# The opening of a two-layer trunk: scale's modulation units first, four separate signals, shift's units last

## The chip, the cores and the metric

The kernel runs on one core of a Trainium2 chip. The metric is the device time of one execution in microseconds; the time of a kernel is the median of its runs. The profile shows one execution, instruction by instruction.

## What is computed

The reference is a two-layer trunk (model width 1024) over 256 context and 256 latent tokens. What matters here is how each layer begins:

```python
mod = jax.nn.silu(c) @ w_mod[i] + b_mod[i]
mod_c = jax.nn.silu(c_ctx) @ w_mod[i] + b_mod[i]
sh1, sc1, g1, sh2, sc2, g2 = jnp.split(mod[:, None, :], 6, axis=-1)
h = _modulate(_rmsnorm(x, norm1_g[i]), sh1, sc1)      # h * (1 + scale) + shift
...
y, yc = _mixer(h, hc, ...)                            # begins with h @ w_in[i]
x = x + g1 * y
...
x = x + g2 * _peer(h2, ...)                           # 128*128 experts
```

So the first projection of layer 0 needs the RMS of x (a mean of squares over the 1024 channels of each token), the scale sc1 (which goes into the gain) and the shift sh1. w_mod of a layer is 1024 x 6144 floats. The kernel holds it as 24 units of 1 MB, four to each of the six parts: units 0 to 3 give sh1, units 4 to 7 give sc1.

## The kernel before

All weights come through `ring`, four slots of 1 MB each. Unit u goes into slot u % 4. SyncE (SP) issues every load in program order; ahead of the load of unit u it waits until the slot's `used` counter says that the unit before it in that slot has been read by TensorE. Each slot has its own arrival signal, `unit_in`. The stages follow each other in one list: `mod`, `norm1`, `front`, `s5`, `ret`, `merge`, `norm2`, `route`, `gates`, `experts`, twice, and `final`. The change touches `mod` and the first `norm1`.

Before, SP issues three loads on one signal, `const_in`: `cst` (378.5 KB), `par` (188 KB: biases, gains, the two condition vectors, the S5 parameters) and `xT` (2 MB). TensorE, ScalarE and VectorE all start by waiting for 48, that is for all three. Then SP streams w_mod units 0 to 7 (`stream`, L648), the last four behind the slots' `used`.

The engines in stage `mod`, layer 0, in their program order:

- **ScalarE**: silu of the condition (L1552) and its copy into `cond0` (L1529); eight squares of `xT` into `hT` (`squares`, L1481); an Exp chain of small parameter operations with VectorE (L1555 to L1563), which needs three loads of function tables; the Sqrt of the mean (`stddev`, L1487); then `mod_rows`, which copies the row of each modulation unit out of PSUM into `mrow0` (L1536), eight copies.
- **TensorE**: `norm_mean`, eight products with a matrix of 1/1024 (16 instructions of 512 columns, two for each product) into PSUM bank 7; `mod_rows`, for each of eight units eight products (16 instructions of 256 columns) into bank k; `mod_columns`, 16 products (32 instructions of 2 columns) that turn the rows of shift and scale into columns in bank 4.
- **VectorE**: the small parameter chain (L2042 to L2077); `inverted`, the reciprocal of the deviations in `rs1` (L1987); `mod_tables`, which adds the bias (L2006) and makes the gain out of the scale (L2012, L2013).

Stage `norm1` and the first unit of `front` then run as a pipeline over the eight channel blocks k:

- **VectorE** scales in place (`normed`, L1998, two instructions to a block, signal `h_scaled`), subtracts for the low part of the first weight unit (`front_low`, L2021), and makes the low part of h (`loP`, L2087).
- **ScalarE** first copies the first front unit to its rounded form (`front_high`, L1515), then adds the shift (`shifted`, L1499, output `hiP`, signal `h_ready`).
- **TensorE** makes the first projection in three parts: high weights by `hiP` as its blocks come, low weights by `hiP`, high weights by `loP`. Its last instruction frees the front unit's slot.

In `front` SP's loads interleave: one front unit, two late modulation units, and so on, each into a slot that TensorE must have freed. Every load, and every wait, behind this point hangs on the events before it; none is tied to an absolute time.

`count(eng, s, n)` waits for a semaphore with a credit that VectorE adds at its start (4 for `mod_row`), so a row's bank can be written before a copy was made.

Of the kernel before, what the change touches and what calls it, by code (L numbers as in the profile page):

```python
# [22 lines left out]
P = 128  # L23
DM = 1024
# [158 lines left out]
def x_for(st, k):  # L183

    if st[0] == "norm2":
        return X_COUNT[st] - OUT_UNITS + k // 2 + 1 if st[2] else X_COUNT[st]
    return X_COUNT[st] - KD + k + 1
# [7 lines left out]
def passes_done(st):  # L195

    return sum(s[0] == "experts" for s in STAGES[:STAGES.index(st)])
# [30 lines left out]
def norms_before(st):  # L228
    return [s for s in STAGES if s[0] in ("norm1", "norm2", "final")].index(st)
# [28 lines left out]
def build_program(nc, a, until=None):  # L258
    stages = STAGES if until is None else STAGES[:until]
    ctx = ExitStack()  # L260
    with ctx:
# [3 lines left out]
        def sem(name):  # L265
            return ctx.enter_context(nc.semaphore(name))
# [205 lines left out]
        ps = ctx.enter_context(nc.psum_tensor("ps", [P, 8, 512], F32))  # L472


        const_in = sem("const_in")
        unit_in = [sem(f"unit_in{s}") for s in range(RING)]
        u_in = [sem(f"u_in{s}") for s in range(RING)]
        keys_in = sem("keys_in")
# [104 lines left out]
        def count(eng, s, n):  # L583

            eng.wait_ge(s, n + CREDIT[s.name])
# [45 lines left out]

        @block.sync
        def _(sp):
            sp.dma_start(cst[:, :], a["consts"]).then_inc(const_in, 16)
            sp.dma_start(par[:, :], a["params"]).then_inc(const_in, 16)
            sp.dma_start(xT[:, :, :], a["x_t"]).then_inc(const_in, 16)

            def load(u, src, i=None, per=0):
                n = u // RING
# [8 lines left out]
            def stream(u, src, count):  # L648

                head = RING if u < RING else 0  # L650
                for k in range(head):
                    load(u + k, src[k])
                turns_ = (count - head) // RING
                with sp.Fori(0, turns_) as i:
                    for k in range(RING):
                        load(u + head + k, src[bass.ds(i * RING + (head + k), 1)].rearrange("o p n -> (o p) n"), i, RING)
# [43 lines left out]
            for st in stages:  # L700
                kind, l, h = st
                u = BASE[st]
                if kind == "mod":
                    stream(u, a["w_mod"][0, 0:EARLY], EARLY)
                elif kind == "front":
                    for k in range(FRONT_UNITS):
                        load(u + front_at(l, k), a["w_front"][l, k])
# [176 lines left out]

        @block.tensor
        def _(pe):
            pe.wait_ge(const_in, 48)

            def mm(out, w, x, start, stop, **k):
                return pe.matmul(out, w, x, start=start, stop=stop, **k)  # L890
# [1 line left out]
            def norm_mean(st, sqb, w):  # L892
                n = norms_before(st)
                for k in range(KD):

                    pe.wait_ge(sq_ready, KD * n + k + 1)
                    last = mm(ps[:, mean_bank(st), 0:w], cst[:, C_ONES_D:C_ONES_D + P], sqb[:, k, :], k == 0, k == KD - 1)
                last.then_inc(mean_ready, 1)
# [13 lines left out]
            def mod_rows(u, l, first, n, bank, cond):  # L912

                with pe.Fori(0, n // RING) as i:
                    for k in range(RING):
                        mod_row_of(u + k, l * MOD_UNITS + first + k, bank + k, cond, i)

            def mod_columns(l, s0, s1, row, bank, begin=0):

                count(pe, mod_row, l * MOD_UNITS + MOD_UNITS // 6 * s1)  # L920
                for c in range(s0 * KD, s1 * KD):
                    at = (c - begin * KD) * P
                    last = mm(ps[:, bank, 2 * c:2 * c + 2], row[:, at:at + P], cst[:, C_SEL:C_SEL + 2], True, True)
                last.then_inc(mod_col, 1)

            for st in stages:
                kind, l, h = st
                u = BASE[st]
                if kind == "mod":


                    norm_mean(("norm1", 0, 0), hT, TL)
                    pe.wait_ge(cond_ready, 1)
                    mod_rows(u, 0, 0, EARLY, 0, cond0)
                    mod_columns(0, 0, 2, mrow0, 4)
                elif kind == "norm1" and l:
                    norm_mean(st, sq1, TL)
                elif kind == "norm2":
# [531 lines left out]
        @block.scalar  # L1470
        def _(act):
            own = Chain(act, act_own)
            act.wait_ge(const_in, 48)

            def squares(st, sqb, lo, w):
                for k in range(KD):
                    if st != STAGES[1]:
                        act.wait_ge(x_ready, x_for(st, k))
                    if k == KD // 2 and passes_done(st):
                        act.wait_ge(x_back, 16 * passes_done(st))  # L1480
                    act.activation(sqb[:, k, :], xT[:, k, lo:lo + w], ACT.Square).then_inc(sq_ready, 1)  # L1481

            def stddev(st, rs, w):
                n = norms_before(st)

                act.wait_ge(mean_ready, n + 1)
                act.activation(rs[:, 0:w], ps[:, mean_bank(st), 0:w], ACT.Sqrt, bias=eps).then_inc(std_ready, 1)  # L1487

            def shifted(st, dst, w, lo, row):

                n = norms_before(st)
                for k in range(KD):
                    act.wait_ge(h_scaled, KD * n + k + 1)
                    for hf in range(w // 256):
                        side = hf if w > 256 else lo // CTX
                        s = slice(hf * 256, hf * 256 + 256)
                        d = dst[:, k, s]
                        src = d if row else by_four_of(scaled(st[1], k, s))
                        last = act.activation(d if row else by_four(hiP[:, k, :], s), src, ACT.Identity,  # L1499
                                              bias=modT[:, st[1], row, k, side:side + 1])  # L1500
                    last.then_inc(h_ready, 1)
# [46 lines left out]
            for st in stages:  # L1548
                kind, l, h = st
                u = BASE[st]  # L1550
                if kind == "mod":
                    own.link(act.activation(par[:, N_C:N_C + 16], par[:, N_C:N_C + 16], ACT.Silu))  # L1552
                    filled(cond0, 1)
                    squares(("norm1", 0, 0), hT, 0, TL)
                    own.link(act.activation(lg[:, :], par[:, N_DEC:N_DEC + 16], ACT.Exp))  # L1555
                    own.link(act.activation(lg[:, :], lg[:, :], ACT.Copy, scale=-1.0))

# [3 lines left out]
                    act.activation(sp_(S_SIN), sp_(S_T1), ACT.Sin)  # L1561
                    act.activation(sp_(S_COS), sp_(S_T2), ACT.Sin, scale=-1.0,
                                   bias=cst[:, C_HPI:C_HPI + 1]).then_inc(s5_trig, 1)  # L1563
                    stddev(("norm1", 0, 0), rs1, TL)
                    mod_rows(u, mrow0, 0, EARLY, 0)
                elif kind == "norm1":
                    if l:
                        squares(st, sq1, 0, TL)
# [10 lines left out]
                elif kind == "front":  # L1579
# [32 lines left out]
                            act.activation(pmag, pmag, ACT.Exp)  # L1612
                            act.activation(r8[:, :], s5p[:, S_LR, l * NG:(l + 1) * NG], ACT.Exp, scale=8.0).then_inc(pow_trig, 1)
                    if l == 0:
                        act.wait_ge(mod_col, 2)
                        act.activation(mcol[:, :], ps[:, 6, 2 * 2 * KD:2 * 5 * KD], ACT.Copy).then_inc(mod_out, 1)
                elif kind == "s5":
                    lo, hi = layer_width(l)
# [356 lines left out]
        def _(dve):  # L1975
            own = Chain(dve, dve_own)
            link = own.link
            v = nc.vector
            dve.wait_ge(const_in, 48)
            for s_ in (mod_row, gate_ready, gate_ps, w_ready):  # L1980
                dve.sem_inc(s_, CREDIT[s_.name])

# [1 line left out]
            def inverted(st, rs, w):  # L1984

                dve.wait_ge(std_ready, norms_before(st) + 1)
                link(v.reciprocal(rs[:, 0:w], rs[:, 0:w]))  # L1987

            def normed(st, rs, w, dst, lo, gains, done):

                if st != ("norm1", 0, 0):
                    inverted(st, rs, w)
                for k in range(KD):
                    for hf in range(w // 256):
                        side = hf if w > 256 else lo // CTX
                        s_ = slice(hf * 256, hf * 256 + 256)
                        d = dst[:, k, s_] if dst is not None else scaled(st[1], k, s_)
                        last = v.scalar_tensor_tensor(d, xT[:, k, lo + hf * 256:lo + hf * 256 + 256],  # L1998
                                                      gains(k, side), rs[:, s_], ALU.mult, ALU.mult)
                    last.then_inc(done, 1)  # L2000
# [34 lines left out]
            for st in stages:  # L2035
                kind, l, h = st
                u = BASE[st]
                if kind == "mod":
# [36 lines left out]
                    link(v.tensor_tensor(sp_(S_T1), sp_(S_COS), li, ALU.mult))  # L2075
                    link(v.tensor_tensor(sp_(S_T0), sp_(S_T0), sp_(S_T1), ALU.subtract))
                    link(v.tensor_tensor(sp_(S_BI), sp_(S_T0), sp_(S_T2), ALU.mult))  # L2077
                    inverted(("norm1", 0, 0), rs1, TL)
                    mod_tables(0, 0, 2, ps[:, 4, 0:4 * KD], 1)
                elif kind == "norm1":  # L2080
                    normed(st, rs1, TL, None, 0, lambda k, s: gain[:, l, 0, k, s:s + 1], h_scaled)
                    front_low(l, 0)
# [57 lines left out]
                elif kind == "s5":  # L2140
# [69 lines left out]

                    def skips():

                        dve.wait_ge(mod_col, 2)
                        v.tensor_tensor(dsk[:, :, :], cst[:, C_DIAG:C_DIAG + 16].unsqueeze(1).to_broadcast([P, 16, 16]),
                                        par[:, N_D:N_D + 16].unsqueeze(2).to_broadcast([P, 16, 16]), ALU.mult).then_inc(d_ready, 1)

# [60 lines left out]
                elif kind == "ret":  # L2277
# [84 lines left out]
                    out_low(1)  # L2362
                    if l == 0:
                        dve.wait_ge(mod_out, 1)
                        mod_tables(0, 2, 5, mcol[:, :], 2)
                elif kind == "merge":
                    lo, hi = layer_width(l)
                    w_ = hi - lo
# [32 lines left out]
                elif kind == "route":  # L2401
# [72 lines left out]
                                               nth[:, 0:k, c].unsqueeze(1).to_broadcast([P, 2, k, hw]), ALU.is_equal)  # L2474
                    link(last)
                    if next_route(st):
                        mod_tables(0, 5, 6, ps[:, 3, 10 * KD:12 * KD], 3)
                        mod_tables(1, 0, 2, ps[:, 2, 0:4 * KD], 4)
                        normed(next_route(st), rs2, 256, h2T, 0, lambda k, s: gain[:, l, 1, k, s:s + 1], h_scaled)
                    tops = topf[:, :, :, :, :].rearrange("p s k t h -> p (s k) (t h)").unsqueeze(2)  # L2480
                    late_ = eq[:, :, :, hw:2 * hw].rearrange("p s k (j m) -> p (s k) j m", j=TOPK // 2)
# [34 lines left out]
                    half = next_mod(st)  # L2516
                    if half:
                        s0, s1 = MOD_PARTS[st]
                        mod_tables(1, s0, s1, ps[:, 2, 2 * s0 * KD:2 * s1 * KD], 4 + half)
                elif kind == "gates":  # L2520
                    gb = groups_before(st)
                    idxT = peer_tiles(l)[1]
# [259 lines left out]
```

## Time and profile before

| | us |
|---|---|
| median of 3 runs | 2964.58 |
| lowest, highest | 2958.05, 2966.55 |
| profiled execution, its own time | 2967.0 |
| its span, first to last instruction | 2965.2 |

Of the span TensorE is busy 92 per cent, VectorE 83, ScalarE 48, GpSimd 16. The profiled execution's own time stands 1.8 us over its span. Starts in the rows further down are counted from the span's start. "SPq" is SyncE's queue with its DMA issues, "PEld" the load of weights into TensorE. A figure in square brackets is the engine's idle time ahead of the row and what ended it.

### The profile page before, as it was taken

The page shows a single profiled execution, that of the slowest core. Times are in us where ns is not written, and L with a number is a line of the kernel's source. Part 1 is how long each engine was busy: PE and PEld are TensorE (multiplying, and loading weights), DVE is VectorE, ACT ScalarE, POOL GpSimd, SP SyncE. Part 2 cuts the span into 40 slices and gives each one's busy share as a digit, 9 for nine tenths or more (in the row PEclk, how much of TensorE's full clock was granted, in tenths as well). Part 3 has the DMA queues.
Part 4 walks back from the last instruction along what each step waited for, and adds up shares of the span by engine and source line. Part 5 has one row for each costly group of instructions (what it writes and reads, how often), then busy time and mean ns, then how long its engine had stood idle before and what let it go on. Part 6 is the DMA issues. An engine that isn't in the chain of part 4 may idle for free.

```text
span 2965.2 us, 52211 instructions
## 1 busy us (share of the span) xinstructions
PE 2722.8 (92%) x18013; PEld 2336.5 (79%) x18013; DVE 2465.5 (83%) x4723; ACT 1417.0 (48%) x2304; POOL 476.6 (16%) x432
## 2 busy tenths in 40 slices
PE   6999999777899999999999998999856999999998
PEld 5778877556788888887888886887846888888887
DVE  5477654998898989889999997786699898889887
ACT  4343432217754444445454545224416666666664
POOL 0000000005432323222333220000005010100010
PEclk9999999878999999999999999999978999999999
DMA  6522222644499999998999992432430788888885
GB/s 249 210 93 81 105 100 100 241 156 167 173 346 344 351 343 345 349 350 331 347 341 344 342 333 106 135 102 80 171 128 29 256 313 316 316 312 319 314 321 207
DMA packets 170583, 709.29 MB, mean 239 GB/s; under 512 B 16848, under 2 KB 48752, under 8 KB 123120
## 3 DMA queue, kind: packets, MB, share of 16 engines
q1 hardware_dynamic: 132128, 430.02, 39.8%
q0 software_dynamic: 38352, 277.92, 26.0%
q8 instruction: 61, 1.00, 0.1%
q14 instruction: 42, 0.34, 0.0%
HBM read 691.13 MB, written 16.65 MB: 239 GB/s over the span
## 4 chain that ended last, share of the span: by engine, by line
PE 75%; DVE 14%; DMA 4%; ACT 3%; SPq 2%; issue 2%; DVEq 0%; ACTq 0%; POOL 0%
PE ps L890 74%; DVE hot L2538 2%; DMA ring<-in_experts 2%; SPq L670 2%; DVE hot L2533 1%; DVE hot L2536 1%; DMA ring<-in_w_mod 1%; DVE loP L2087 1%; DMA gate_scratch<-spill 1%; DVE topi L2422 0%; DVE topi L2430 0%; DVE sc L2424 0%; DVE gst L2239 0%; PE ps L1027 0%; DMA ring<-in_w_front 0%
## 5 line engine op out<-in xcount | busy, mean ns | idle before, releaser
L815 POOL DMA_INDIRECT gbuf<-in_expert_rows,gidx x192 | 277.5, 1445 | 1336.8 <-DVE yg L2591 1228.6
L890 PE MATMUL ps<-h2a,ehi 128*128 128x320 f32 x2048 | 453.3, 309 | 2.6 <-DVE elo L2548 2.6
L1947 ACT ACTIVATE ehi<-ring 128x1024 fp32r<-128x1024 f32 x256 | 271.5, 1061 | 253.3 <-PE ps L890 247.8
L890 PEld LDWEIGHTS ps<-h2a,ehi 128*128 128x128 f32 x2048 | 348.6, 188 | 21.4 <-DVE elo L2548 3.6
L890 PE MATMUL ps<-h2b,ehi 128*128 128x192 f32 x2048 | 348.2, 273 | 1.8 <-DVE elo L2548 1.8
L2603 DVE TENSOR_TENSOR elo<-ring,ehi 128x1024 fp32r<-128x1024 f32 x256 | 312.8, 1222 | 33.9 <-ACT ehi L1947 33.7
L2548 DVE TENSOR_TENSOR elo<-ring,ehi 128x1024 fp32r<-128x1024 f32 x256 | 311.9, 1219 | 30.9 <-ACT ehi L1912 30.9
L890 PEld LDWEIGHTS ps<-h2b,ehi 128*128 128x128 f32 x2048 | 321.3, 192 | 13.3 <-DVE elo L2548 2.1
L890 PE MATMUL ps<-h2a,elo 128*128 128x320 f32 x1024 | 316.9, 309 | 0.0
L1912 ACT ACTIVATE ehi<-ring 128x1024 fp32r<-128x1024 f32 x256 | 268.9, 1051 | 29.7 <-DMA ring<-in_experts 29.7
L890 PE MATMUL ps<-h2b,elo 128*128 128x192 f32 x1024 | 281.7, 275 | 0.0
L2591 DVE SCALAR_TENSOR_TENSOR yg<-gbuf,gw,yg 128x1024 f32<-128x1024 f32 x192 | 245.8, 1280 | 28.1 <-ACT gw L1934 28.1
L890 PE MATMUL ps<-ehi,whA 128*128 128x512 f32 (+1 forms) x768 | 244.5, 400 | 20.3 <-DVE wlA L2627 20.3
L890 PE MATMUL ps<-ehi,wlA 128*128 128x512 f32 (+1 forms) x768 | 241.2, 396 | 0.0
L890 PE MATMUL ps<-ehi,wB 128*128 128x512 f32 x768 | 241.1, 395 | 0.0
L890 PE MATMUL ps<-elo,whA 128*128 128x512 f32 (+1 forms) x768 | 240.3, 394 | 0.0
L2581 DVE SCALAR_TENSOR_TENSOR gbuf<-gbuf,h2n 128x1024 f32<-128x1024 f32 x192 | 234.0, 1219 | 0.0
L890 PEld LDWEIGHTS ps<-h2b,elo 128*128 128x128 f32 x1024 | 197.2, 193 | 0.0
L890 PEld LDWEIGHTS ps<-h2a,elo 128*128 128x128 f32 x1024 | 192.7, 188 | 0.0
L890 PE MATMUL ps<-hot 128*128 128x128 f32 x1024 | 140.4, 292 | 35.4 <-ACT hot L1899 28.9
L890 PEld LDWEIGHTS ps<-elo,whA 128*128 128x128 f32 (+1 forms) x768 | 132.8, 173 | 47.8 <-issue 0.4
L890 PEld LDWEIGHTS ps<-ehi,wlA 128*128 128x128 f32 (+1 forms) x768 | 132.4, 172 | 45.4
(443 smaller groups left out, 5467.8 us busy)
## 6 DMA issues: line engine op xcount, KB each, us to landing
ring<-in_experts SPq DMA_DIRECT2D x512, 512.0 KB, 5.8
ring<-in_w_mod SPq DMA_DIRECT2D x48, 1024.0 KB
ring<-in_w_side SPq DMA_DIRECT2D x24, 1024.0 KB
ring<-in_w_front SPq DMA_DIRECT2D x12, 1024.0 KB
ring<-in_w_merge SPq DMA_DIRECT2D x16, 768.0 KB
ring<-in_w_q SPq DMA_DIRECT2D x12, 1024.0 KB
gate_scratch<-spill SPq DMA_DIRECT2D x40, 256.0 KB, 2.0
gateA<-gate_scratch SPq DMA_DIRECT2D x4, 2560.0 KB
```

What stands on the lines that cost most here:

```text
L670: sp.dma_start(ring[:, e % RING, 0:DM], src[:, 0:DM]).then_inc(u_in[e % RING], 16)
L815: pool.indirect_dma_start(gbuf[:, k % 2, :], None, a[f"expert_rows{l}"], bass.IndirectOffsetOnAxis(gidx[:, at:at + 1], 0)).then_inc(gather ...
L890: return pe.matmul(out, w, x, start=start, stop=stop, **k)
L1912: act.activation(ehi[:, k % 2, :], ring[:, (u + k) % RING, 0:DM], ACT.Copy).then_inc(uhi_ready, 1)
L1947: act.activation(ehi[:, 2 + k % 2, :], ring[:, (u + k) % RING, DM:2 * DM], ACT.Copy).then_inc(vhi_ready, 1)
L2087: last = v.scalar_tensor_tensor(by_four(loP[:, k, :], s_), by_four_of(scaled(l, k, s_)), modT[:, l, 0, k, side:side + 1], by_four(hiP[:, k ...
L2533: v.tensor_tensor(hot[:, g, 1, 0:2, :], row.unsqueeze(1).to_broadcast([P, 2, P]), idxT[:, 1, 4 * n:4 * n + 2].unsqueeze(2).to_broadcast([P ...
L2538: v.tensor_tensor(hot[:, g, 0, :, :], row.unsqueeze(1).to_broadcast([P, 4, P]), idxT[:, 0, 4 * n:4 * n + 4].unsqueeze(2).to_broadcast([P, ...
L2548: v.tensor_tensor(elo[:, r, 0:DM], ring[:, r, 0:DM], ehi[:, k % 2, :].bitcast(F32), ALU.subtract).then_inc(ulo_ready, 1)
L2581: v.scalar_tensor_tensor(rows, rows, 1.0, h2n[:, :], ALU.mult, ALU.mult, accum_out=ga[:, at]).then_inc(dot_ready, 1)
L2591: v.scalar_tensor_tensor(yg[:, :], gbuf[:, n % 2, DM:2 * DM], gw[:, at], yg[:, :], ALU.mult, ALU.add).then_inc(acc_done, 1)
L2603: v.tensor_tensor(elo[:, r, DM:2 * DM], ring[:, r, DM:2 * DM], ehi[:, 2 + b, :].bitcast(F32), ALU.subtract).then_inc(vlo_ready, 1)
```

## The change

It does this:

1. `par` is loaded ahead of `cst`, each with its own signal; `xT` is loaded in two halves of 1 MB (channel blocks 0 to 3 and 4 to 7), each with its own signal, behind the first four modulation units. ScalarE and VectorE start at `cst` and `par`, TensorE at `cst`; only `squares` waits for a half.
2. The four units of the scale (w_mod 4 to 7) come first, those of the shift (0 to 3) last, behind `xT`.
3. TensorE's order becomes: four rows of the scale, eight of its columns (bank 4), the mean of the squares, four rows of the shift, its eight columns (bank 5). The loops become straight code.
4. ScalarE's order becomes: silu, `cond0`, the Exp chain, four row copies of the scale, the squares, the Sqrt, four row copies of the shift. `shifted` waits for the shift's table.
5. VectorE makes the gain's table at the end of `mod`, the reciprocal at the start of `normed`, and the shift's table between blocks 2 and 3 of `normed`.
6. The counts of later waits on `mod_col` and `mod_done` go up by one.

```diff
-            sp.dma_start(cst[:, :], a["consts"]).then_inc(const_in, 16)
-            sp.dma_start(par[:, :], a["params"]).then_inc(const_in, 16)
-            sp.dma_start(xT[:, :, :], a["x_t"]).then_inc(const_in, 16)
+            sp.dma_start(par[:, :], a["params"]).then_inc(par_in, 16)
+            sp.dma_start(cst[:, :], a["consts"]).then_inc(cst_in, 16)
...
                 if kind == "mod":
-                    stream(u, a["w_mod"][0, 0:EARLY], EARLY)
+                    for k in range(MOD_W):
+                        load(u + k, a["w_mod"][0, MOD_W + k])
+                    for n in range(2):
+                        part = slice(n * KD // 2, (n + 1) * KD // 2)
+                        sp.dma_start(xT[:, part, :], a["x_t"][:, part, :]).then_inc(x_in[n], 16)
+                    for k in range(MOD_W):
+                        load(u + MOD_W + k, a["w_mod"][0, k])
...
         def _(pe):
-            pe.wait_ge(const_in, 48)
+            pe.wait_ge(cst_in, 16)
...
+                    def part_columns(s, rows, bank):
+
+                        count(pe, mod_row, rows)
+                        for c in range(s * KD, (s + 1) * KD):
+                            last = mm(ps[:, bank, 2 * c:2 * c + 2], mrow0[:, c * P:c * P + P], cst[:, C_SEL:C_SEL + 2], True, True)
+                        last.then_inc(mod_col, 1)
+
+                    pe.wait_ge(cond_ready, 1)
+                    for k in range(MOD_W):
+                        mod_row_of(u + k, k, k, cond0)
+                    part_columns(1, MOD_W, 4)
                     norm_mean(("norm1", 0, 0), hT, TL)
-                    pe.wait_ge(cond_ready, 1)
-                    mod_rows(u, 0, 0, EARLY, 0, cond0)
-                    mod_columns(0, 0, 2, mrow0, 4)
+                    for k in range(MOD_W):
+                        mod_row_of(u + MOD_W + k, MOD_W + k, k, cond0)
+                    part_columns(0, 2 * MOD_W, 5)
...
         def _(act):
-            act.wait_ge(const_in, 48)
+            act.wait_ge(cst_in, 16)
+            act.wait_ge(par_in, 16)
...
                     if st != STAGES[1]:
                         act.wait_ge(x_ready, x_for(st, k))
+                    elif k % (KD // 2) == 0:
+                        act.wait_ge(x_in[k // (KD // 2)], 16)
...
                 n = norms_before(st)
+                if st == ("norm1", 0, 0):
+                    act.wait_ge(mod_done, 2)
                 for k in range(KD):
                     act.wait_ge(h_scaled, KD * n + k + 1)
...
                     filled(cond0, 1)
-                    squares(("norm1", 0, 0), hT, 0, TL)
...
+                    def rows_of(part, first):
+
+                        for k in range(MOD_W):
+                            unit_used(act, u + first + k)
+                            at = DM * part + 256 * k
+                            act.activation(mrow0[:, at:at + 256], ps[:, k, 0:256], ACT.Copy).then_inc(mod_row, 1)
+
+                    rows_of(1, 0)
+                    squares(("norm1", 0, 0), hT, 0, TL)
                     stddev(("norm1", 0, 0), rs1, TL)
-                    mod_rows(u, mrow0, 0, EARLY, 0)
+                    rows_of(0, MOD_W)
...
-            dve.wait_ge(const_in, 48)
+            dve.wait_ge(cst_in, 16)
+            dve.wait_ge(par_in, 16)
...
-                if st != ("norm1", 0, 0):
-                    inverted(st, rs, w)
+                inverted(st, rs, w)
                 for k in range(KD):
+                    if st == ("norm1", 0, 0) and k == 3:
+                        mod_tables(0, 0, 1, ps[:, 5, 0:2 * KD], 2)
...
-                    inverted(("norm1", 0, 0), rs1, TL)
-                    mod_tables(0, 0, 2, ps[:, 4, 0:4 * KD], 1)
+                    mod_tables(0, 1, 2, ps[:, 4, 2 * KD:4 * KD], 1)
```

## Rows read from the trace of the kernel before

**Rows 1.** The page: the span and the shares of the engines.
```profile
span 2965.2 us, 52211 instructions
```
**Rows 2.** The chain of waits from 0 to 80 us: start, length, what.
```profile
1.65 9.69 DMA xT<-in_x_t
...
25.61 9.64 DMA ring<-in_w_mod
...
50.23 9.57 DVE loP L2087 x16
...
62.51 10.50 DMA ring<-in_w_front
```
**Rows 3.** Opening by engines, 5 us each: length, busy (x count), clock, DMA, GB/s.
```profile
0.00:5.00 5.00, 0.00 (x0) 0.00 (x0) 0.00 (x0) 1.28 (x1) 0.19 (x4) 1.00 0.56 185
5.00:10.00 5.00, 0.00 (x0) 0.00 (x0) 0.00 (x0) 0.00 (x0) 0.00 (x0) 1.00 0.94 357
10.00:15.00 5.00, 1.91 (x3) 0.90 (x4) 0.27 (x1) 3.00 (x8) 0.00 (x0) 1.00 1.01 426
15.00:20.00 5.00, 5.00 (x11) 2.13 (x10) 1.18 (x6) 3.55 (x8) 0.00 (x0) 1.00 0.92 390
...
30.00:35.00 5.00, 3.39 (x32) 1.15 (x32) 2.32 (x1) 0.77 (x2) 0.00 (x0) 0.66 1.01 428
```
**Rows 4.** SyncE's timeline (start, length) and the DMA issues' landing times (last number).
```profile
2.12 23.81 SPq L646 DMA_DIRECT2D ring<-in_w_mod  x8
...
par<-in_params SPq DMA_DIRECT2D x1, 188.0 KB, 2.9
```
**Rows 5.** Timeline of TensorE up to the end of the first front unit.
```profile
13.09 8.86 PE L890 MATMUL ps<-hT,cst 128*128 128x512 f32 x16 [13.09 <-ACT hT L1481]
...
21.89 3.66 PE L890 MATMUL ps<-ring,cond 128*32 128x256 f32 x64
...
30.42 1.94 PE L890 MATMUL ps<-ring,cond 128*32 128x256 f32 x16 [1.42 <-DMA ring<-in_w_mod]
...
35.37 1.07 PE L890 MATMUL ps<-ring,cond 128*32 128x256 f32 x16 [1.03 <-DMA ring<-in_w_mod]
...
37.03 3.82 PE L890 MATMUL ps<-cst,mrow 128*128 128x2 f32 x32 [0.59 <-ACT mrow L1536]
...
51.52 3.93 PE L890 MATMUL ps<-elo,hiP 128*128 128x256 f32 x32
...
59.84 0.73 PE L890 MATMUL ps<-wX,loP 128*128 128x256 f32 x4 [0.42 <-DVE loP L2087]
```
**Rows 6.** Tile cst, its readers: shortest, median and longest in ns.
```profile
L890 PE MATMUL ps<-hT,cst x16: 592/592/1191, 13.1 to 21.4; 128*128 128x512 f32 x16
```
**Rows 7.** Timeline of ScalarE and VectorE up to the first front unit.
```profile
12.34 4.25 ACT L1481 ACTIVATE hT<-xT 128x512 f32<-128x512 f32 x8
...
18.39 0.26 ACT L1558 ACTIVATE s5w<-par 128x64 f32<-128x64 f32 x1
...
26.06 0.69 ACT L1487 ACTIVATE rs<-ps,cst 128x512 f32<-128x512 f32 x1
...
28.71 0.22 DVE L2077 TENSOR_TENSOR s5p<-s5w 128x64 f32<-128x64 f32 x1
...
28.97 3.35 DVE L1987 RECIPROCAL rs<-rs 128x512 f32<-128x512 f32 x1
...
36.59 0.38 ACT L1536 ACTIVATE mrow<-ps 128x256 f32 x1 [1.71 <-PE ps L890]
...
37.76 1.91 ACT L1515 ACTIVATE wX<-ring 128x2048 fp32r<-128x2048 f32 x1 [0.78 <-DMA ring<-in_w_front]
...
41.60 6.42 DVE L1998 SCALAR_TENSOR_TENSOR xT<-xT,gain,rs 128x256 f32<-128x256 f32 x16
42.52 8.38 ACT L1499 ACTIVATE hiP<-xT,modT 128x256 fp32r<-128x256 f32 x16 [2.85 <-DVE xT L1998]
...
47.94 2.28 DVE L2021 TENSOR_TENSOR elo<-ring,wX 128x2048 fp32r<-128x2048 f32 x1
```

More of the change, by code:

```diff
@@ L472, in build_program @@
         ps = ctx.enter_context(nc.psum_tensor("ps", [P, 8, 512], F32))
-        const_in = sem("const_in")
+        cst_in, par_in = sem("cst_in"), sem("par_in")
+        x_in = [sem(f"x_in{k}") for k in range(2)]
         unit_in = [sem(f"unit_in{s}") for s in range(RING)]
@@ L1614, in _ @@
                     if l == 0:
-                        act.wait_ge(mod_col, 2)
+                        act.wait_ge(mod_col, 3)
                         act.activation(mcol[:, :], ps[:, 6, 2 * 2 * KD:2 * 5 * KD], ACT.Copy).then_inc(mod_out, 1)
@@ L2211, in skips @@
                     def skips():
-                        dve.wait_ge(mod_col, 2)
+                        dve.wait_ge(mod_col, 3)
                         v.tensor_tensor(dsk[:, :, :], cst[:, C_DIAG:C_DIAG + 16].unsqueeze(1).to_broadcast([P, 16, 16]),
@@ L2364, in _ @@
                         dve.wait_ge(mod_out, 1)
-                        mod_tables(0, 2, 5, mcol[:, :], 2)
+                        mod_tables(0, 2, 5, mcol[:, :], 3)
                 elif kind == "merge":
@@ L2476, in _ @@
                     if next_route(st):
-                        mod_tables(0, 5, 6, ps[:, 3, 10 * KD:12 * KD], 3)
-                        mod_tables(1, 0, 2, ps[:, 2, 0:4 * KD], 4)
+                        mod_tables(0, 5, 6, ps[:, 3, 10 * KD:12 * KD], 4)
+                        mod_tables(1, 0, 2, ps[:, 2, 0:4 * KD], 5)
                         normed(next_route(st), rs2, 256, h2T, 0, lambda k, s: gain[:, l, 1, k, s:s + 1], h_scaled)
@@ L2518, in _ @@
                         s0, s1 = MOD_PARTS[st]
-                        mod_tables(1, s0, s1, ps[:, 2, 2 * s0 * KD:2 * s1 * KD], 4 + half)
+                        mod_tables(1, s0, s1, ps[:, 2, 2 * s0 * KD:2 * s1 * KD], 5 + half)
                 elif kind == "gates":
```

## The prediction

> **What bounds the opening now.** The change touches only the first 60 us of a span of 2965.2 us [rows 1], so I read three views of that part: the chain of waits, then the DMA rate beside it, then the engines' timelines.
>
> The chain [rows 2] starts with xT, which lands at 11.34 (1.65 + 9.69), since all three compute engines wait for cst, par and xT together. Then TensorE makes the mean of the squares, 8.86 us from 13.09, and behind it four modulation rows until 25.55 [rows 5]. Next comes a wait of 9.64 us for a modulation unit [rows 2], the last such unit being used at 35.37 [rows 5]. Then follow 32 column instructions (3.82 us), the tables, the in-place scaling (from 41.60), and beside it the shift in ScalarE, 42.52 to 50.90 [rows 5, 7]. The low part of h ends at 59.80 [rows 2], and TensorE ends the first front unit at 60.57 [rows 5]. That last moment is what I count to.
>
> The rates [rows 3] show why the modulation wait exists. From 0 to 20 us the DMA engines moved 5 x (185 + 357 + 426 + 390) = 6.79 MB (GB/s times us gives KB). What had been issued is 0.58 MB of cst and par, 2.10 of xT and 4 x 1.05 of units, 6.87 MB together. So everything in the ring was there at about 20 us, and the queue then ran dry, because SP waits for slots [rows 4] that TensorE frees only after the mean, from 22.8 to 25.6 (3.66 us for four units [rows 5]). From there units land 2.45 us apart, 1.05 MB at 428 GB/s [rows 3], the last at 35.37 and the first front unit at 37.76 [rows 5, 7].
>
> Behind 60.57 nothing has an absolute time: the next front unit waits 10.50 us for a load issued at 62.51 [rows 2], once a slot is free. Earlier slots move it as much, so I carry the gain at 60.57 whole to the end.
>
> **The change, part by part.**
>
> *Order of bytes.* The same bytes flow, in another order. I read the moved MB off rows 3 (0.93 at 5 us, 2.71 at 10, 4.84 at 15, 6.79 at 20) and add 0.75 us for the landing, a choice between 0.4 and 1.4: xT's 2.68 MB were through, in order, at 9.9, and it landed at 11.34. par and cst land at about 4.1, by par's 2.9 us [rows 4]. Scale units: 1.63, 2.68, 3.73 and 4.77 MB, so about 8.3, 11.0, 13.1 and 15.6. Halves of xT: 18.0 and 20.5. TensorE frees the four slots as units arrive (10 to 17 us), all before 20, so the shift's units are in the queue when it would have run dry. They follow at 427 GB/s: 22.9, 25.4, 27.8, 30.25. The first front unit lands at 32.7, where it landed at 37.76. SP's waits delay nothing else: the only loads queued behind them are these.
>
> *The small chain* between ScalarE and VectorE runs from 18.39 to 28.93 [rows 7], 10.5 us, behind the squares. Ahead of them, with its first table load, it starts at about 7.0 and ends at 17.5. The four scale copies follow its Sin at about 13.4. Copies 0 to 2 cost nothing, covered by the wait for the last scale unit; without that cover they are 0.38 each [rows 7].
>
> *Scale rows and columns.* A row is 0.92 us (3.66/4) at full rate or 1.94 at the low one [rows 5]. The last ends at 16.6 (17.6 low), its copy 0.45 later, and eight columns are 1.92 (half of 3.82): done at 19.0. The low bound is 21.9, with columns at double length. Which clock? In 30:35 the granted clock was 0.66 on average [rows 3], where rows of this very kind stood between gaps: one took 1.94, the last 1.07 [rows 5]. So bursts raised it again within two units. I take full rate from the third unit on.
>
> *The mean.* Squares of half 0 run from 18.1, of half 1 from 20.6 to 22.8 (0.53 each, 4.25/8 [rows 7]). TensorE starts at 19.0 and needs 8 x 0.86 = 6.9 at full rate; before it took 8.86, its longest instruction being 1191 ns beside a median of 592 [rows 6], a cold start. It would end at 25.9 warm; I take 26.5, with 29.7 as the low bound (columns and four more us at half rate).
>
> *Behind the mean.* Sqrt (0.69) to 27.3, reciprocal (3.35) to 30.7, blocks 0 to 2 of the scaling (3 x 0.80, from 6.42) to 33.1. TensorE meanwhile makes shift rows 0 to 2 and, at 30.25, the last: 31.2. Copy to 31.65, eight columns to 33.6, one short table to 33.9. So VectorE waits about 0.8 us for the shift's columns, continues with blocks 3 to 7 until 37.9 and makes the low weights (2.28) until 40.2.
>
> *ScalarE* holds the first front unit's copy behind the shift's row copies: 32.7 + 1.91 = 34.65. Only then comes the shift, behind the table (33.9) too. It takes 8.38 [rows 7] until 43.1. TensorE's tail then: before, 32 instructions of the low weights started 0.62 behind the last hiP (50.90, 51.52) and took 3.93 [rows 5]; another 32 by loP take about the same, so 8.3 in all, 51.4. loP starts at 40.2 and ends at 49.8 (9.57 [rows 2]); with 0.75 for the last products that is 50.5, so TensorE's own work ends last.
>
> **Sum**: 60.57 - 51.4 = 9.2 us gained. Check by steps: shift starts 34.65 for 42.52, 7.9 us; loP no longer last, 1.3 us. The profiled execution's own 2967.0 (1.8 over the span) would become 2957.8. It stood 2.4 over the median of the runs, 2964.58, so for the median: **2955.4**.
>
> The bounds: with the mean ending at 29.7, Sqrt 30.5, reciprocal 33.9, table and blocks 0 to 2 36.5, shift to 44.9, TensorE to 53.2: 7.3 gained. With landings 0.7 sooner (lag 0.4, shift table at 33.2) at best 9.9.
>
> **The rivals.**
>
> *A slip that stays inside the measurement.* The mean is now late on TensorE, behind the scale's columns. Up to 27.9 it costs nothing; beyond, each us costs one. Half-rate stretches between 8 and 20 us, where TensorE has one row in 2.5 us, speak for it; that the clock rose again under just such rows speaks against [rows 3, 5]. It gives 7.3 to 8.5 gained, 2956 to 2957.5. The DMA engines matter too: the last front wait of 10.50 us [rows 2] is more than three units' 7.4.
>
> The Trainium skill, DMA: Bandwidth & Descriptors, section on queues, rings and completion order, says each of the engines that share a transfer reports by itself and that completion is not first in, first out. By that rule the lag of 0.75 may grow with ten transfers queued; the trace's xT lag of 1.4 agrees that it can.
>
> *The order of bytes is not what I take it for.* If transfers in one queue share the engines, so that scale units and xT land together at 20, then rows end at 23.7, columns at 26, the mean at 33, shift starts at 39.2: 55.9, or 4.7 gained, 2959.9. Against it: units land evenly 2.45 us apart [rows 3, 5], and xT lands first.
>
> *The clock stays low for the whole opening* (the one that ends slower). TensorE's work before was one block of 12.5 us; now it is rows with gaps. If every instruction up to the front unit's end is at half rate: scale columns end at 21.9, the mean takes 13.7 to 35.6, shift rows 7.8 to 43.4, copy and columns to 47.7, shift 48.0 to 56.4, tail 16.6 to 73.0: 12.4 lost, 2977. It decides once the end passes 60.57; with a warm tail it is 64.7, 4.1 lost. Against it: TensorE left its cold start during the mean itself (median 592 ns [rows 6]), and rows 5's 1.07 came after gaps.
>
> [...]
>
> **How the numbers follow.** About 0.3 per cent, 8.9 us, is what a measurement of this kernel can tell from no change. My forecast of 9.2 lies just above it, so signs of both kinds are near. Forecast: 0.55. Slip: 0.27. Shared order: 0.08. Low clock: 0.06. The rest, 0.04, is anything unforeseen in either direction. The forecast's case ends over 8.9 about four times in five once the runs' scatter (8.5 us between lowest and highest) is added, and the slip sometimes: faster 0.48, same 0.45, slower 0.07. The forecast's own range is 2951 to 2959, from gains of 7.3 to 9.9 and 3 us for the median's scatter; to take in the shared order it reaches to 2964, and down to 2949 for a fast session.
>
> **What would show it.** Right: DMA above 400 GB/s without a gap from 10 to 33 us; mean from about 19 to 26.5; first front unit's copy at 32.7; scaling done at 38; shift from 34.7; TensorE ending the front unit at 51.4, behind hiP and not loP; everything later as far apart as before. Wrong: a gap in the DMA rate near 20 us (slots freed late), rows at 1.94 throughout, a mean past 28, a shift that starts behind its table rather than the front copy, or a stage behind 60 us that is longer than it was.

## The result and the profile after

The changed kernel takes 2947.07 us in the median of 7 runs (2939.95 to 2953.04), the kernel before 2964.92 in the median of 7 beside it. The ratio is 0.9942, interval 0.9926 to 0.9957: 17.9 us faster, where the forecast was 9.2 and the range ended at 2949. Further runs settle the size better. In a second series the changed kernel had 2951.36 (ratio 0.9959, 0.9944 to 0.9973) beside 2962.12 for the kernel before, 10.8 us. All 14 runs of it have the median 2948.83. The kernel before has the medians 2964.92, 2962.12, 2962.50 and 2963.11 in four series (7, 18, 27 and 35 runs); I take the last. So the change brings about 14 us, and a fifth of the first figure was scatter.

The page after, beside [rows 1]:

```profile
span 2941.7 us, 52190 instructions
```

The chain of waits from 0 to 80 us, start, length and what, beside [rows 2]:

```profile
3.07 13.53 DMA ring<-in_w_mod
16.64 1.85 PE ps L896 x16
...
18.95 11.66 PE ps L896 x48
...
30.63 4.71 DMA ring<-in_w_front
...
37.18 8.35 ACT hiP L1521 x16
...
45.58 10.25 PE ps L896 x100
...
55.84 9.18 DMA ring<-in_w_front
```

The wait for xT and the wait of 9.64 us for a modulation unit are gone. The chain now runs through the scale's units, one block of TensorE (columns and mean) and the front unit's load. The 5 us stretches (columns as in [rows 3]) show the queue:

```profile
15.00:20.00 5.00, 3.94 (x38) 1.84 (x30) 2.37 (x10) 1.65 (x4) 0.00 (x0) 1.00 1.00 424
20.00:25.00 5.00, 5.00 (x15) 2.58 (x15) 0.52 (x3) 4.69 (x8) 0.00 (x0) 0.66 1.01 419
25.00:30.00 5.00, 5.00 (x23) 2.04 (x25) 0.00 (x0) 0.49 (x2) 0.00 (x0) 1.00 0.95 393
30.00:35.00 5.00, 4.50 (x72) 2.98 (x65) 4.57 (x5) 1.83 (x5) 0.00 (x0) 1.00 0.71 261
```

There is no gap at 20 us any more, as forecast. But there is a new one at 30 to 33 (261 GB/s), which the forecast didn't have. TensorE's timeline of the opening says why, beside [rows 5]:

```profile
9.36 1.93 PE L896 MATMUL ps<-ring,cond 128*32 128x256 f32 x16 [9.36 <-DMA ring<-in_w_mod]
...
11.69 1.94 PE L896 MATMUL ps<-ring,cond 128*32 128x256 f32 x16 [0.40 <-DMA ring<-in_w_mod]
...
14.16 1.94 PE L896 MATMUL ps<-ring,cond 128*32 128x256 f32 x16 [0.53 <-DMA ring<-in_w_mod]
...
16.64 1.80 PE L896 MATMUL ps<-ring,cond 128*32 128x256 f32 x16 [0.55 <-DMA ring<-in_w_mod]
...
20.76 8.81 PE L896 MATMUL ps<-hT,cst 128*128 128x512 f32 x16
...
29.50 3.66 PE L896 MATMUL ps<-ring,cond 128*32 128x256 f32 x64
```

All four rows took about double the 0.92 us of full rate, though the granted clock column says 1.00 up to 20 us (it shows the low level, 0.5, from 21.6 to 25 only; the mean of that stretch is the 0.66 above). The mean took 8.81 us and ended at 29.5, not 26.5. So the first slot came free at 30.6, after the queue had run dry, and the front unit's copy started at 35.4 rather than 32.7. The rest of the opening, beside [rows 7]:

```profile
30.40 3.35 DVE L2018 RECIPROCAL rs<-rs 128x512 f32<-128x512 f32 x1 [8.79 <-ACT rs L1507]
...
33.78 2.46 DVE L2030 SCALAR_TENSOR_TENSOR xT<-xT,gain,rs 128x256 f32<-128x256 f32 x6
...
35.36 1.91 ACT L1537 ACTIVATE wX<-ring 128x2048 fp32r<-128x2048 f32 x1 [1.75 <-DMA ring<-in_w_front]
...
37.18 8.34 ACT L1521 ACTIVATE hiP<-xT,modT 128x256 fp32r<-128x256 f32 x16
...
42.53 9.64 DVE L2118 SCALAR_TENSOR_TENSOR loP<-xT,modT,hiP 128x256 fp32r<-128x256 f32 x16
...
53.85 1.93 PE L896 MATMUL ps<-ring,cond 128*32 128x256 f32 x32
```

The last row is the first work behind the first front unit. It starts at 53.85, where the row of the same kind started at 60.51 before: 6.7 us. The spans differ by 23.5. So in this pair of profiles 16.8 us were gained behind the part that the change touches, and the study was about that.

To see where, I lined up ScalarE's instructions of two traces from the end backwards (they are the same ones behind the opening) and took the difference of their starts. From the opening to 765 us it stays between 6 and 11. It rises by 2.3 at 765 to 800, by 9.1 in the layer-0 experts stage (800 to 1440), mostly where the gates' parts are loaded back, and by 2.8 between 1800 and 2140.

### The profile page after: what moved, and what is told of

Same layout as the page of the kernel before. It is cut to its first block, busy times and chain, and to the rows that moved or that the text cites. A ratio compares the mean times of both kernels' runs of the same rounds, so it can differ in the third digit from the quotient of the medians.

```text
span 2941.7 us, 52190 instructions
## 1 busy us (share of the span) xinstructions
PE 2720.7 (92%) x18013; PEld 2335.1 (79%) x18013; DVE 2465.6 (84%) x4724; ACT 1414.6 (48%) x2304; POOL 478.0 (16%) x432
## 4 chain that ended last, share of the span: by engine, by line
PE 76%; DVE 13%; DMA 6%; ACT 3%; issue 2%; SPq 1%; DVEq 0%; POOL 0%; ACTq 0%; POOLq 0%
PE ps L896 75%; DMA ring<-in_experts 3%; DVE hot L2569 2%; DMA ring<-in_w_mod 2%; DVE hot L2564 1%; DVE hot L2567 1%; DMA ring<-in_w_front 1%; DMA gate_scratch<-spill 1%; SPq L670 1%; DVE gst L2270 0%; DVE elo L2053 0%; DVE rs L2018 0%; DVE loP L2118 0%; PE ps L1044 0%; ACT hiP L1521 0%
## 5 line engine op out<-in xcount | busy, mean ns | idle before, releaser
L2634 DVE TENSOR_TENSOR elo<-ring,ehi 128x1024 fp32r<-128x1024 f32 x256 | 312.6, 1221 | 29.8 <-ACT ehi L1977 29.7
L2579 DVE TENSOR_TENSOR elo<-ring,ehi 128x1024 fp32r<-128x1024 f32 x256 | 311.7, 1218 | 23.5 <-ACT ehi L1942 23.5
```

What stands on the lines that cost most here:

```text
L2579: v.tensor_tensor(elo[:, r, 0:DM], ring[:, r, 0:DM], ehi[:, k % 2, :].bitcast(F32), ALU.subtract).then_inc(ulo_ready, 1)
L2634: v.tensor_tensor(elo[:, r, DM:2 * DM], ring[:, r, DM:2 * DM], ehi[:, 2 + b, :].bitcast(F32), ALU.subtract).then_inc(vlo_ready, 1)
```

## Experiments

**Both kernels again.** Is the late gain real, or scatter of single executions?

```diff
(no edit; the kernel before, the changed kernel)
```

> The kernel before, unchanged, for a second trace of it. Theory A (the part of the gain that lies behind the opening, some 9 us between the medians, is real and belongs to the changed program): its layer-0 experts stage shows the same stalls at the gate loads as the first trace of before, within 2 us of its length. Theory B (it is scatter between single executions): the length of that stage differs by 5 us or more between the two traces of the same kernel. Ratio to before 1.000 within 0.002.

> The changed kernel, unchanged, for a second trace and a second median. Both theories: ratio 0.9925 to 0.9957, and the first front unit ends at 53.9 within 0.5 us. Theory A: the experts stage of layer 0 is 9 us shorter than in both traces of before. Theory B: it is as long as in one of the two traces of before.

> A third trace of the kernel before, for the scatter of the late stages and of the opening: the end of the first front unit between 60.5 and 64, the time from 765 us on within 7 us of the other two traces.

Measured: before again 2963.13 (ratio 1.0, 0.999 to 1.0011) and one run of 2961.94; the changed kernel 2951.36 (0.9959). Both theories are partly right. Against the first trace of before, the experts stage of layer 0 (800 to 1440 us) is 3.3 and 5.4 us shorter in the other two traces of before, and 9.1 and 6.3 us shorter in the two of the changed kernel. Behind 765 us the three traces of before differ by 7 us among themselves (6.9 and 5.5 under the first one), so the first profile was a long one there. But the changed kernel's second trace was 10.7 under it too, and 14.3 us lie between the medians.

The opening scatters as well, and most of it is the clock. In the first trace of before the 32 column instructions took 3.82 us [rows 5], with a granted clock of 1.00 from 38 to 40 us. In the next two the granted clock was 0.50 from 40 to 44 us, and the columns were slower by 2.4:

```profile
38.00 6.29 PE L890 MATMUL ps<-cst,mrow 128*128 128x2 f32 x32 [0.59 <-ACT mrow L1536]
```
```profile
38.57 6.17 PE L890 MATMUL ps<-cst,mrow 128*128 128x2 f32 x32 [0.59 <-ACT mrow L1536]
```

The first front unit ended at 63.95 and 64.41 there, not 60.5. Three experiments below keep this opening's work and order and have 63.87, 64.49 and 65.19: of six executions the median is 64.2. The changed kernel's two have 53.85 and 56.41, mean 55.1; the second lies well outside the 53.9 within 0.5 that I expected, since its mean ended at 31.9. So the opening's typical gain is 9.1 us, and 5.2 of the 14.3 are left for the late part. With two traces on one side, either figure may be off by a microsecond or so.

**The mean's place and the clock.**

```diff
 # mean_first: xT's halves ahead of the units, squares and mean first
+                    norm_mean(("norm1", 0, 0), hT, TL)
                     pe.wait_ge(cond_ready, 1)
...
-                    norm_mean(("norm1", 0, 0), hT, TL)
 # warm: idle products on TensorE
+                    filler(6)
                     pe.wait_ge(cond_ready, 1)
                     for k in range(MOD_W):
                         mod_row_of(u + k, k, k, cond0)
+                        filler(2 if k < MOD_W - 1 else 1)
```

> The change with one part undone: the halves of xT are loaded ahead of the modulation units and the squares and the mean come first on ScalarE and TensorE, as before; own signals and the scale-then-shift order stay. If the forecast's miss in the opening (53.9 in place of 51.4) is the late mean, which held the slots and so the first front unit's load, the front copy starts at 32.7 to 33.2 in place of 35.4 and the first front unit ends at 51.3 to 51.8, 2.3 us sooner than in the changed kernel. The rival (the queue itself gives that landing) says 35.4 and 53.9 again. Time: 2 us under the changed kernel, or the same.

> The changed kernel with idle products of 256 columns on TensorE ahead of and between the scale's rows (6, 2, 2, 2 and 1 of them, into a bank nobody reads), so that the engine isn't at the low clock when the mean begins. If the clock made the mean late, the four rows take 0.93 us each in place of 1.94, the mean takes 6.9 us in place of 8.8 and ends at 26.5 to 27.3 in place of 29.5, and the first front unit ends at 51.6, 2.3 us sooner. If the clock is not the cause, the mean ends at 29.5 again and the time is that of the changed kernel.

Measured: mean_first 2948.35 (0.9954, 0.9939 to 0.997), warm 2946.62 (0.9942, 0.9925 to 0.9959), neither separable from the changed kernel. The mean moved as theory said, the end hardly did. In warm the rows took 1.07 to 1.15 us, the mean took 7.11 and ended at 27.3:

```profile
20.25 7.11 PE L896 MATMUL ps<-hT,cst 128*128 128x512 f32 x16
...
31.91 1.07 PE L896 MATMUL ps<-ring,cond 128*32 128x256 f32 x16 [1.39 <-DMA ring<-in_w_mod]
...
33.49 3.29 PE L896 MATMUL ps<-cst,mrow 128*128 128x2 f32 x16 [0.50 <-ACT mrow L1597]
```

So the low clock did make the mean late. But the last shift unit was now awaited until 31.9, the columns behind it took 3.29 in place of 2.16 (granted clock 0.50 from 34 to 36 us), and the shift started at 37.03 (37.18 in the changed kernel), behind its own table. The first front unit ended at 53.76, not at the 51.6 expected. The landings are a second reason: with slots free early, the last shift unit still landed 1.6 us behind the forecast's 30.25, and the front unit's copy started at 34.40, not 32.7. In mean_first the mean ended at 18.6, but ScalarE's small chain held the row copies until 24 to 25; the scale's columns then pushed the shift's rows to 27.7 and into the low clock (5.60 us for three). The front copy started at 36.8, the unit ended at 55.26. My expectation of 51.3 to 51.8 missed that second queue. The order of the change is therefore no worse than these two, and no better.

**Parts of the change.**

```diff
 # signals_only: the kernel before, separate signals, xT in halves in its old place
-            pe.wait_ge(const_in, 48)
+            pe.wait_ge(cst_in, 16)
...
 # no_swap: the changed kernel, shift's units, rows, columns and table first
-                        load(u + k, a["w_mod"][0, MOD_W + k])
+                        load(u + k, a["w_mod"][0, k])
```

> The kernel before with the separate signals alone (par first, then cst, xT in two halves ahead of the units, in the old place; squares, mean, rows and columns in the old order). Theory A (the opening's gain comes from slots freed before the queue runs dry): the mean ends at 18.5 in place of 21.9, the slots are freed from 19.4, the dry stretch shrinks from 4.4 us to about 1.5, the last early unit lands at 32.5 in place of 35.4, and the first front unit ends 2.5 to 3 us sooner than in the kernel before. Rival (only the order of bytes matters): it ends where it did, 60.6 to 64.

> The changed kernel with the parts not swapped: the shift's units, rows and columns first, the scale's last, so that the gain is ready only behind the last unit; all else as changed. If the swap matters, the scaling starts at 36.4 in place of 33.8 and the low part of h ends at 54.7, so the first front unit ends 1.5 us later than in the changed kernel (55.4 for 53.9, at the same clock). If it doesn't, since ScalarE's copy of the front weights comes last anyway, within 0.3 us.

Measured: signals_only 2958.86 (0.9992, 0.998 to 1.0003). Its mean ended at 19.75 (18.5 expected), the columns started at 34.96 for 37.03 to 38.57, and the front unit ended at 60.86, with columns at the low rate (6.25 us); against the two openings of before with slow columns that is 3.3 us. Theory A holds in direction and size, though the total of 3.6 between medians isn't clear of noise by its interval. no_swap 2951.93 (0.9961, 0.9948 to 0.9975): its mean ended later (30.8), the unit at 56.57. Counted from the mean's end the tail is 25.8 us for 24.4 and 24.5 in the two traces of the changed kernel: the swap is worth 1.2 to 1.4, about as expected, and with it undone TensorE's last products wait for the low part of h again, as in the kernel before.

**The late gain without the early one.**

```diff
 # delayed: the changed kernel, 6.9 us of idle products ahead of the third part of the first front unit
+                                    if part == 2 and not l:
+                                        for _i in range(16):
+                                            mm(ps[:, 2, 0:256], cst[:, C_ID:C_ID + P], cst[:, 0:256], True, True)
```

> The changed kernel with 16 idle products of 256 columns on TensorE (0.43 us each, 6.9 us) between the second and the third part of the first front unit, which puts the end of that unit at 60.8 to 63.4, about where the two traces of before have it (60.6 and 64.0). Theory A (the gain is made in the opening alone, all behind it is moved and otherwise scatters): the time is that of the kernel before, ratio 0.998 to 1.001. Theory B (the changed program gains another 5 us or so behind the opening, whatever the opening takes): ratio 0.996 to 0.998, 5 to 10 us under the kernel before.

Measured: 2954.47 (0.9973, 0.9962 to 0.9983), 8.0 us under the kernel before beside it (2962.50). Its front unit ended at 61.25, 2.9 under the typical 64.2. So 5.1 us are gained with most of the early gain taken out: theory B, and the late gain doesn't depend on when the opening ends.

What can a changed opening do at 780 us? The clearest step is the one at 765 to 800, and there the traces fall into two kinds. ScalarE waits for the last spill of the gates ahead of its copy h2x. In the kernel before, then in the changed one:

```profile
787.43 1.06 ACT L1923 ACTIVATE h2x<-gbufX 128x1024 f32<-128x1024 f32 x1 [2.70 <-DMA gate_scratch<-spill]
```
```profile
776.81 1.06 ACT L1953 ACTIVATE h2x<-gbufX 128x1024 f32<-128x1024 f32 x1 [0.37 <-DMA gate_scratch<-spill]
```

In all three traces of before and in signals_only the wait is 2.0 to 2.7 us; in all six of the changed kernel and its variants it is 0.37 or 0.38. The DMA view of the 783 to 788 us stretch of before has this, the queues by kind and the spill with its time to landing:

```profile
q8 instruction: 1, 0.02, 2.4%
...
gate_scratch<-spill SPq DMA_DIRECT2D x1, 256.0 KB, 4.3
```

and the same stretch of the changed kernel (774.7 to 777.5) has no packet of that queue:

```profile
gate_scratch<-spill SPq DMA_DIRECT2D x1, 256.0 KB, 2.0
```

Beside the late spill a 16 KB block of instructions was being loaded, and the spill landed 2.3 us later. The queue has 61 packets of 16 KB in either kernel; in the trace they come at other places of the program. The change made the rows' loop straight code, and TensorE's stream got longer ahead of everything. The Trainium skill, Runtime: NRT & Kernel Launch, section on instruction fetch mechanics, says each engine's instruction memory is refilled in blocks of 16 KiB (256 instructions) by a DMA queue; the packets' size agrees. It calls the cost of a block boundary mostly hidden; here one was not.

**Moving the instruction stream alone.**

```diff
 # straight_pe: the kernel before, TensorE's rows without the loop
-                    mod_rows(u, 0, 0, EARLY, 0, cond0)
+                    for k in range(EARLY):
+                        mod_row_of(u + k, k, k % RING, cond0)
 # straight_act_sp: the same on ScalarE and SyncE alone; straight_all: on all three
 # padded: the changed kernel
+                    for _i in range(128):
+                        pe.sem_inc(pad_sem, 1)
                     pe.wait_ge(cond_ready, 1)
```

> The kernel before with TensorE's eight modulation rows as straight code in place of a loop of four run twice; same work, same order. Theory B2 (the late gain comes from where the blocks of TensorE's instruction stream are loaded: straight rows put some 128 more instructions ahead of everything, so the 16 KB block loads, the queue called instruction, fall at other moments): the last spill lands 2 us after its issue in place of 4.3, ScalarE waits 0.4 us ahead of h2x in place of 2.0 to 2.7, and the time is 4 to 8 us under the kernel before (ratio 0.9973 to 0.9987). Theory A2 (the late gain has to do with the new order): ratio 0.999 to 1.001 and the wait of 2 us or more stays.

> The kernel before with straight code on ScalarE (eight copies) and SyncE (eight loads) alone, TensorE keeps its loop. Theory B2: TensorE's stream lies where it did, the wait ahead of h2x stays at 2.0 to 2.7 us, and the time is that of the kernel before within 2 us; if ScalarE's or SyncE's code is what counts, it is 4 to 8 us under it.

> The kernel before with straight code on all three engines in the opening. Theory B2: as straight_pe, 4 to 8 us under the kernel before. Theory A2: no change.

> The changed kernel with 128 semaphore instructions ahead of TensorE's first row, where the engine waits for the first unit anyway (the opening at most 1 us later). Theory B2: the stream is moved by another 8 KB, together about one block of 16 KB against the kernel before, so the block loads fall about where they fell there: a block load lies in the last spill again, the wait ahead of h2x is back at 2 us or more, and the time is 4 to 8 us over the changed kernel (ratio to before 0.997 to 0.999). Theory A2: the time of the changed kernel, ratio 0.994 to 0.996.

| kernel | median us | ratio to before | interval | front unit ends | wait ahead of h2x |
|---|---|---|---|---|---|
| straight_act_sp | 2960.12 | 0.9990 | 0.9979 to 1.0000 | 65.19 | 1.61 |
| straight_pe | 2958.50 | 0.9989 | 0.9978 to 1.0000 | 64.49 | 0.40 |
| straight_all | 2956.61 | 0.9983 | 0.9970 to 0.9995 | 63.87 | 0.41 |
| delayed | 2954.47 | 0.9973 | 0.9962 to 0.9983 | 61.25 | 0.38 |
| padded | 2963.68 | 1.0008 | 0.9999 to 1.0018 | 64.06 | 2.67 |

delayed stands beside 2962.50 for the kernel before, the others beside 2963.11. With TensorE's rows straight the wait fell to 0.4; with the other two engines alone it was 1.61, and the block load lay beside the spill still. The times alone don't separate these two: straight_act_sp is 3.0 us under the kernel before (within 2 was expected), straight_pe 4.6, and both intervals reach 1.0000. What separates them is the wait, and where in the late part the time is gained, which comes below. The padding brought the wait back to 2.67, and with it the block load in the spill's stretch; the view of padded (785.2 to 789.5):

```profile
q8 instruction: 1, 0.02, 1.4%
```

The padding was a costlier edit than I expected. The opening was to be at most 1 us later, but the 128 semaphore instructions took 15.1 us, as padded's chain has it:

```profile
9.26 15.09 issue
```

They held the scale's slots and put the front unit's end at 64.06, by accident right where before has it. So padded has the changed order, but neither an earlier end of the opening nor the moved stream, and its time is that of the kernel before (0.6 us over it), where 4 to 8 us over the changed kernel was expected. straight_all has before's order and the moved stream, and is 6.5 us under it (interval 1.5 to 8.9). The three estimates of what the stream's place is worth are then 5.1 (delayed), 6.5 (straight_all) and 4.6 (straight_pe), beside the 5.2 left over in the changed kernel.

Where do these 5 us lie? Eight traces have the moved stream (the changed kernel's two, mean_first, warm, no_swap, delayed, straight_pe, straight_all), six have it where the kernel before has it (that kernel's three, signals_only, straight_act_sp, padded). I compared the medians of the two kinds, all lined up with the first trace of before. From 765 us to the end they lie 4.6 us apart. The step at 765 to 800 is 2.1 to 2.4 us with the moved stream and -0.1 to 1.0 in the others: 2.1 between the medians. From 800 to 1800, the loads of the gates with them, both kinds have the same median (4.45). Single traces differ there by up to 9 us, so the 9.1 of the first pair was scatter. Behind 1800 the medians are 4.3 and 0.75.

The first step there is as sharp as the one at the spill. At 1900 to 1905 us all eight gain 1.8 us, and none of the six more than 0.1. The chain of the kernel before, then of the changed one, at the same work:

```profile
1900.32 2.03 PE ps L890 x96
1902.35 1.47 issue
```
```profile
1880.63 2.11 PE ps L896 x101
```

"issue" is time in which the engine waited for nothing that the profile shows. In the six traces TensorE stops for 1.42 to 1.48 us in the middle of one group of products (ps<-gk,xT), and in the eight it doesn't. In the kernel before a 16 KB packet of the instruction queue ran from 1901.6 to 1902.5, just ahead of the stop's end at 1903.8. So TensorE was probably waiting for its own next instructions; that is argued from the two times, not shown.

What stays open: of the 1.8 us, 1.2 are left at 1950, and some 2 us more are gained behind it, where the steps differ from trace to trace and I did not assign them to single waits.

## Why the prediction was wrong

**Right, point by point.** The queue ran without a gap from 10 to 29 us (393 to 424 GB/s in the stretches up to 30), and slots were freed as units landed. The small chain ended at 17.7 (17.5 forecast). The swap was worth 1.2 to 1.4 us, about what the tables' place said. TensorE's own work, not loP, ended the unit: hiP ended at 45.53 and the unit 8.3 us later, the tail taken from [rows 5]. Between 60 and 765 us the work was moved by what the opening gave, 6.7 us at 62 and 8.3 at 764, with single steps of up to 3 on the way.

**The mean** was one mis-sized term inside the opening. I took full rate from the third row on, from one case in [rows 3, 5] where the clock rose between gaps; it stayed low through the fourth row in the first trace (1.94, 1.94, 1.94, 1.80) and through part of the mean. The mean ended at 29.5 and 31.9 in the two traces, so the low bound of 29.7 was nearer than the value of 26.5, and the second trace passed even that.

**The landings** were the other. I took 0.75 us from a transfer's last bytes to its landing. The last scale unit landed at 16.60 (15.6 forecast), the squares of the two halves started at 19.12 and 21.61 (18.0 and 20.5), and in warm, where the mean was early, the front unit's copy started 1.7 us late. So the late mean alone doesn't account for the 2.4 us between 51.4 and 53.85: with it mended, warm still ended at 53.76. A small slip beside it: by the prediction's own figures the first two scale units land at 7.7 and 10.7, not 8.3 and 11.0; nothing hung on these two.

**The base** was wrong by as much the other way. I counted from one execution whose columns ran at full rate (3.82), and took its 2.4 us over the median for the measure of how typical it was. In five of six executions those columns were slow (4.8 to 7.0 us). The typical end is 64.2, not 60.57. These errors cancel: 9.1 measured for 9.2 forecast, by luck.

**The step that failed** is the sentence "Behind 60.57 nothing has an absolute time", which made me carry the opening's gain to the end and no more. It is true of waits, but it left out what the change does to the instruction stream: loops turned into straight code move every later block load. That is worth about 5 us here (5.1, 6.5 and 4.6 in three experiments that change the stream or keep it moved without the early gain), and no rival had it. The forecast's sign of being right, "everything later as far apart as before", failed by 16.8 us in the first pair of profiles. Of the 8.3 us between 2955.4 and 2947.07, some 5 are the gain beyond 9.2, 1.5 the first median of before (2964.58 for 2963.11 over 35 runs), and 1.8 the first seven runs of the changed kernel (2947.07 for 2948.83 over 14). 2948.83 lies just outside the range as well.

## To carry to other kernels

A change of code length on one engine moved all later instruction loads of that engine, and on this kernel of 2963 us that was worth about 5 us, over half of what the reordering gave: compare with a version that has the new code length and the old order before crediting an order. Take two or three profiles before counting from a moment that lies in a stretch with gaps on TensorE; one trace may hold the rare clock. And when a wait is taken away at the front, ask of each freed slot whether its successor is released by something that moved later.

## What the runs showed of the hardware

With the load of one 16 KB block of instructions beside it, the last 256 KB spill took 3.2 to 4.3 us to its landing in six traces; without one it took 2.0 in eight. TensorE stopped for 1.42 to 1.48 us at one place of its program in those six traces, with no semaphore to wait for, and not in the eight. Increments of a semaphore issued by TensorE took 0.118 us each (128 in 15.1 us) with nothing else to do. Short bursts on TensorE (1.94 us of work in every 2.47) stayed at the doubled length for 9 us in one execution, and in another of the same kernel the third burst took 1.07. The granted clock column gives 1.00 from 10 to 15 us in both: at the start of this program the lengths of the rows tell the clock, and that column doesn't.
